# Where the first guess of rstd is made for three RMS norms of a two-layer encoder, and in how many VectorE steps it is refined

## What is computed

```python
def rmsnorm(x, g):
    xf = x.astype(jnp.float32)
    y = xf * lax.rsqrt(jnp.mean(xf * xf, axis=-1, keepdims=True) + EPS)
    return (y * g.astype(jnp.float32)).astype(x.dtype)

for i in range(DEPTH):
    h = rmsnorm(x, norm_mix[i])
    x = x + mixer(h)                       # stick-breaking (i = 0), mLSTM (i = 1)
    h = rmsnorm(x, norm_ffn[i])
    x = x + hierarchical_moe(h, ...)       # top-1 of 4 groups, top-2 of its 8 experts
return rmsnorm(x, norm_final)
```

## Time and profile before

| | us |
|---|---|
| median of 3 runs | 1743.56 |
| lowest and highest | 1743.27, 1744.08 |
| the profiled execution, its own time | 1744.14 |
| its span in the trace | 1742.4 |
| TensorE busy | 1572.3 (90%) |
| VectorE busy | 731.9 (42%) |
| ScalarE busy | 424.3 (24%) |
| mean granted TensorE clock | 0.947 |

### The profile page before, as it was taken

The page is one execution under the profiler, slowest core; times in us unless marked ns, Lnnn a source line. Parts: engine busy times, 40 slices in busy tenths (PEclk is TensorE's granted clock), DMA queues, the critical chain, the costliest instruction groups (busy, mean ns, idle before and its releaser), DMA issues.

```text
span 1742.4 us, 25494 instructions
## 1 busy us (share of the span) xinstructions
PE 1572.3 (90%) x9954; PEld 1080.8 (62%) x9954; DVE 731.9 (42%) x1170; ACT 424.3 (24%) x572; POOL 44.4 (3%) x70
## 2 busy tenths in 40 slices
PE   8999999999997789778899999999999887688776
PEld 8999999888544244324397988988864343234322
DVE  5544444443342233222364857657434332233213
ACT  6344343433000000000154333333320000000002
POOL 0010000100100000000011000000000000000000
PEclk9999999999998998889799999999999998898888
DMA  7645455578999999999954465575799999999996
GB/s 259 212 153 177 153 169 182 209 288 308 381 423 423 426 426 424 425 427 425 412 180 159 154 195 172 165 265 206 252 368 424 426 424 424 427 426 424 425 426 243
DMA packets 160785, 543.88 MB, mean 312 GB/s; under 512 B 17504, under 2 KB 34064, under 8 KB 127824
## 3 DMA queue, kind: packets, MB, share of 16 engines
q1 hardware_dynamic: 151232, 541.12, 79.8%
q10 hardware_dynamic: 9040, 0.49, 0.3%
q0 software_dynamic: 448, 1.36, 0.2%
HBM read 540.83 MB, written 2.10 MB: 312 GB/s over the span
## 4 chain that ended last, share of the span: by engine, by line
PE 68%; DMA 21%; SPq 5%; DVE 2%; issue 1%; ACT 1%; DVEq 0%; ACTq 0%
PE psum_G L755 35%; DMA ring<-in_moe_w 21%; PE psum_S L755 18%; PE psum_A L755 9%; SPq L556 5%; PE psum_T L755 5%; DVE w_lo L434 1%; ACT w_hi L430 1%; PE psum_A L762 0%; DMA x<-in_x 0%; ACT arena L1308 0%; DVE x L1855 0%; DVE h L2108 0%; PE psum_T L1009 0%; PE psum_T L762 0%
## 5 line engine op out<-in xcount | busy, mean ns | idle before, releaser
L755 PE MATMUL psum_A<-ring,arena 128*32 128x512 f32 x1984 | 289.4, 713 | 133.5 <-DMA ring<-in_moe_w 130.8
L434 DVE TENSOR_TENSOR w_lo<-ring,w_hi 128x2048 fp32r<-128x2048 f32 x126 | 289.1, 2298 | 280.5 <-ACT w_hi L430 278.3
L430 ACT CAST w_hi<-ring 128x2048 fp32r<-128x2048 f32 x127 | 241.9, 1906 | 238.5 <-PE psum_G L755 152.2
L755 PEld LDWEIGHTS psum_A<-ring,arena 128*32 128x32 f32 x1984 | 67.2, 120 | 301.6 <-issue 300.4
L1988 DVE COPY arena_two<-psum_A 128x512 f32<-128x512 f32 x64 | 44.3, 692 | 365.7 <-PE psum_T L755 336.3
L2020 DVE TENSOR_TENSOR x<-x,psum_S 128x512 f32<-128x512 f32 x128 | 88.0, 688 | 166.8 <-PE psum_S L755 166.8
L755 PE MATMUL psum_G<-xT_hi,w_hi 128*128 128x256 f32 x512 | 149.5, 292 | 0.0
L755 PE MATMUL psum_G<-xT_hi,w_lo 128*128 128x256 f32 x512 | 145.0, 283 | 0.0
L755 PE MATMUL psum_G<-xT_lo,w_hi 128*128 128x256 f32 x512 | 145.0, 283 | 0.0
L1517 ACT ACTIVATE arena<-psum_T 128x64 f32<-128x64 f32 x64 | 14.4, 224 | 473.4 <-PE psum_T L755 473.4
L755 PE MATMUL psum_G<-arena,h 128*128 128x128 f32 x1024 | 126.8, 284 | 0.0
(11 more groups left out here) (244 smaller groups left out, 2150.6 us busy)
## 6 DMA issues: line engine op xcount, KB each, us to landing
ring<-in_moe_w SPq DMA_DIRECT2D x368, 1024.0 KB, 19.1
ring<-in_ml_w_in SPq DMA_DIRECT2D x48, 1024.0 KB, 5.1
ring<-in_sb_w_in SPq DMA_DIRECT2D x47, 1024.0 KB, 5.1
ring<-in_sb_w_out SPq DMA_DIRECT2D x16, 1024.0 KB, 5.0
turned_slots<-in_moe_w SPq DMA_DIRECT2D x16, 1024.0 KB, 13.2
ring<-in_ml_w_out SPq DMA_DIRECT2D x16, 1024.0 KB, 5.1
x<-in_x SPq DMA_DIRECT2D x4, 512.0 KB, 8.2
out_x<-h SPq DMA_DIRECT2D x4, 512.0 KB, 2.7
```

The costliest lines, as they stand in the source:

```text
L430: act.copy(w_hi[:, slot_place(j), :], ring[:, slot_place(j), :]).then_inc(hi_made, 1)
L434: dve.tensor_tensor(w_lo[:, slot_place(j), :], ring[:, slot_place(j), :], w_hi[:, slot_place(j), :].bitcast(F32), ALU.subtract).then_inc(l ...
L755: return pe.matmul(dst, lhsT, rhs, start=start, stop=stop, skip_group_check=True)
```

## The change

Three tiles and one semaphore are new. For norms 1, 3 and 4:

- `early_mean(n, cols)` sums the first three chunks as before and writes two tiles: `mean_early` = sum / 2048 + eps and `half_early` = -0.5 * sum / 2048 - 0.5 * eps, and signals `early_ready`. It is now done for norm 4 as well, ahead of VectorE's last two additions.
- ScalarE makes the seed without VectorE: `seed_of_last` computes Ln(sumsq_c[:, b, 3] / 2048 + mean_early[:, b]), with the activation's scale and bias, one block at a time, right behind the square of that block, and `seed_end` takes Exp of both blocks. It no longer waits for `mean_ready`.
- VectorE writes `minus_half` = -0.5 * (mean + eps) from the last chunk and `half_early`.

For all five norms the Newton step is newton[:, b] = rstd * minus_half * rstd (one operation for each block, with `minus_half[:, b]` as a scalar for each partition; the two don't depend on each other), then rstd = (newton + 1.5) * rstd. Before it was two dependent operations on both blocks and then the last. Norms 0 and 2 keep the old hand-over to ScalarE, with one more VectorE operation for `minus_half` ahead of it.

```diff
-                if n not in (1, 3):
-                    squares_end()
-                act.wait_ge(mean_ready, n + 1)
+                squares_end()
+                act.wait_ge(mean_ready, n // 2 + 1)
                 act.activation(rstd[:, :], mean_eps[:, :], ACT.Ln)
+                seed_end()
+
+            def seed_end():
+
                 act.drain()
                 act.activation(rstd[:, :], rstd[:, :], ACT.Exp, scale=-0.5).then_inc(rstd_seed, 1)
+
+            def seed_of_last(n, b, c):
+
+                act.wait_ge(early_ready, {1: 1, 3: 2, 4: 3}[n])
+                act.activation(rstd[:, b:b + 1], sumsq_c[:, b, c:c + 1], ACT.Ln, scale=1.0 / D,
+                               bias=mean_early[:, b:b + 1])
...
             def make_rstd(n):
 
-                if n in (1, 3):
-                    dve.wait_ge(squares_done, n + 1)
-                    dve.scalar_tensor_tensor(out=mean_eps[:, :].unsqueeze(2), in0=sumsq_c[:, :, XC - 1:XC], scalar=1.0 / D,
-                                             in1=newton[:, :].unsqueeze(2), op0=ALU.mult, op1=ALU.add)
+                dve.wait_ge(squares_done, n + 1)
+                if n in (1, 3, 4):
+                    last = XC - 1
+                    dve.scalar_tensor_tensor(out=minus_half[:, :].unsqueeze(2), in0=sumsq_c[:, :, last:last + 1],
+                                             scalar=-0.5 / D, in1=half_early[:, :].unsqueeze(2), op0=ALU.mult, op1=ALU.add)
                 else:
...
+                    dve.tensor_scalar(minus_half[:, :], sumsq[:, :], -0.5 / D, -0.5 * EPS, ALU.mult, ALU.add)
+                    dve.drain().then_inc(mean_ready, 1)
+                dve.drain()
                 dve.wait_ge(rstd_seed, n + 1)
-                dve.tensor_tensor(newton[:, :], rstd[:, :], mean_eps[:, :], ALU.mult)
-                dve.drain()
-                dve.scalar_tensor_tensor(out=newton[:, :], in0=newton[:, :], scalar=-0.5, in1=rstd[:, :],
-                                         op0=ALU.mult, op1=ALU.mult)
+                for b in range(TB):
+                    dve.scalar_tensor_tensor(out=newton[:, b:b + 1], in0=rstd[:, b:b + 1], scalar=minus_half[:, b:b + 1],
+                                             in1=rstd[:, b:b + 1], op0=ALU.mult, op1=ALU.mult)
                 dve.drain()
                 dve.scalar_tensor_tensor(out=rstd[:, :], in0=newton[:, :], scalar=1.5, in1=rstd[:, :],
                                          op0=ALU.add, op1=ALU.mult)
...
                     for dc in range(4):
+                        if layer == 1 and not more and dc == XC - 1:
+                            early_mean(2, dc)
```

More of the change, by code:

```diff
@@ L193, in build @@
         newton = sb("newton", [P, TB])
+        mean_early = sb("mean_early", [P, TB])
+        half_early = sb("half_early", [P, TB])
+        minus_half = sb("minus_half", [P, TB])
         extra_f = sb("extra_f", [1, 1])
@@ L326, in build @@
         mean_ready = sem("mean_ready")
+        early_ready = sem("early_ready")
         rstd_seed = sem("rstd_seed")
@@ L1444, in last_chunk @@
                     sum_squares(b, c)
+                    if b == TB - 1:
+                        squares_end()
                     if b == 0:
@@ L1448, in last_chunk @@
                                  ).then_inc(emptied["A0"], 1)
-                squares_end()
+                    seed_of_last(2 * layer + 1, b, c)
+                seed_end()
             def first_small_loads(j):
@@ L1542, in quad @@
                                     sum_squares(b, c, moe_squares)
+                                    if c == XC - 1:
+                                        if b == TB - 1:
+                                            squares_end()
+                                        seed_of_last(4, b, c)
+                                if c == XC - 2:
+                                    act.drain().then_inc(squares_early, 1)
+                                if c == XC - 1:
+                                    seed_end()
                 with act.Fori(0, NQUAD - 1) as i:
@@ L1571, in _ @@
                 group("out", NGROUP - 1, NGROUP)
-                rstd_seed_of(2 * layer + 1)
                 experts(layer)
-            rstd_seed_of(4)
         @block.vector
@@ L1579, in make_rstd @@
             def make_rstd(n):
-                if n in (1, 3):
-                    dve.wait_ge(squares_done, n + 1)
-                    dve.scalar_tensor_tensor(out=mean_eps[:, :].unsqueeze(2), in0=sumsq_c[:, :, XC - 1:XC], scalar=1.0 / D,
-                                             in1=newton[:, :].unsqueeze(2), op0=ALU.mult, op1=ALU.add)
-                else:
-                    dve.wait_ge(squares_done, n + 1)
-                    dve.tensor_reduce(sumsq[:, :].unsqueeze(2), sumsq_c[:, :, :], AX, ALU.add)
+                dve.wait_ge(squares_done, n + 1)
[3 more added lines that the diff above has]
+                                             scalar=-0.5 / D, in1=half_early[:, :].unsqueeze(2), op0=ALU.mult, op1=ALU.add)
+                else:
+                    dve.tensor_reduce(sumsq[:, :].unsqueeze(2), sumsq_c[:, :, 0:XC], AX, ALU.add)
                     dve.drain()
                     dve.tensor_scalar(mean_eps[:, :], sumsq[:, :], 1.0 / D, EPS, ALU.mult, ALU.add)
-                dve.drain().then_inc(mean_ready, 1)
+                    dve.tensor_scalar(minus_half[:, :], sumsq[:, :], -0.5 / D, -0.5 * EPS, ALU.mult, ALU.add)
+                    dve.drain().then_inc(mean_ready, 1)
+                dve.drain()
                 dve.wait_ge(rstd_seed, n + 1)
-                dve.tensor_tensor(newton[:, :], rstd[:, :], mean_eps[:, :], ALU.mult)
-                dve.drain()
-                dve.scalar_tensor_tensor(out=newton[:, :], in0=newton[:, :], scalar=-0.5, in1=rstd[:, :],
-                                         op0=ALU.mult, op1=ALU.mult)
+                for b in range(TB):
+                    dve.scalar_tensor_tensor(out=newton[:, b:b + 1], in0=rstd[:, b:b + 1], scalar=minus_half[:, b:b + 1],
+                                             in1=rstd[:, b:b + 1], op0=ALU.mult, op1=ALU.mult)
                 dve.drain()
@@ L1602, in make_rstd, with early_mean @@
                 dve.drain().then_inc(rstd_ready, 1)
-            def early_mean(layer):
-                dve.wait_ge(squares_early, layer + 1)
-                dve.tensor_reduce(sumsq[:, :].unsqueeze(2), sumsq_c[:, :, 0:XC - 1], AX, ALU.add)
+            def early_mean(n, cols):
+                dve.wait_ge(squares_early, n + 1)
+                dve.tensor_reduce(sumsq[:, :].unsqueeze(2), sumsq_c[:, :, 0:cols], AX, ALU.add)
                 dve.drain()
-                dve.tensor_scalar(newton[:, :], sumsq[:, :], 1.0 / D, EPS, ALU.mult, ALU.add)
-                dve.drain()
+                dve.tensor_scalar(mean_early[:, :], sumsq[:, :], 1.0 / D, EPS, ALU.mult, ALU.add)
+                dve.tensor_scalar(half_early[:, :], sumsq[:, :], -0.5 / D, -0.5 * EPS, ALU.mult, ALU.add)
+                dve.drain().then_inc(early_ready, 1)
             def scaled_lo(layer, units):
@@ L1683, in common_step @@
                         if k == XC - 1:
-                            early_mean(layer)
+                            early_mean(layer, XC - 1)
                         add_chunk(layer, k)
```

## The result

The changed kernel takes 1758.64 us (median of 4 runs, 1757.56 to 1759.10), the kernel before 1743.82 (1743.27 to 1744.22) beside it: a ratio of 1.0082, with a 95% interval of 1.0070 to 1.0093. It is 15 us slower where 1 us less was forecast. The norms do about what was expected of them; the loss is elsewhere, in the stream of the experts' weights.

What follows compares the result with a forecast made beforehand. The chain of waits was taken as TensorE for 68% and DMA for 21% of the span. Norm 3's 0.50 and norm 4's 0.44 us summed to 0.94, from the median 1743.56 to 1742.6, range 1741.4 to 1744.2.

Steps and rivals of the forecast that it cites:

- The step that failed: Expert weight stream behind norm 3: loads are issued 0.50 us earlier and the whole stream ends 0.50 earlier, at 424 GB/s.
- four rivals: Norm 1 pays too 0.20 (1742.1); stall 0.14 (1743.1); half clock at norm 3 0.10 (1744.0); last quad 0.08 (1740 or 1745.5).
- three signs of being wrong: Pair of small operations over 0.5 us; fillers holding TensorE at norm 3; a later stream gap giving the half microsecond back.
- Norms 1 and 3, the rstd chain: From mean_eps or minus_half to the last Newton operation: 0.56 us less than 1.20, ends 0.47 and 0.73.
- The limit behind it: Norm 3, rstd to first experts: router product and fillers limit the gain to 0.50 us, between 0.35 and 0.54.
- Norm 1: TensorE is late behind its fillers at half clock, so cost and gain are 0 in this execution.
- Norm 4: Last square to output operations: 0.54 us less, 0.10 taken off for block 0's Ln, giving 0.44, ends 0.25 and 0.70.
- Sum: Gains over all norms: 0 + 0.50 + 0 + 0 + 0.44 = 0.94 us.
- The clock rivals: Full clock at norm 1: 0.5 us more gained, 1742.1, chance 0.20; half clock at norm 3: +0.46, 1744.0, chance 0.10.

Runs made afterwards that it cites:

- e2: The changed kernel with its three new tiles allocated behind the last one (arena), so older tiles lie where they lay before; 1743.12 us, ratio 0.9987.
- e1: The kernel before with three unused 64-byte tiles ahead of extra_f, moving h, xT, the ring and arenas by 192 bytes; 1758.09 us, ratio 1.0070.
- e3_after_again: The changed kernel measured once more without an edit, beside the kernel before; 1757.12 us, ratio 1.0076.
- e4: The kernel before with one unused 64-byte tile, a shift of 64 bytes; 1759.01 us, ratio 1.0079.
- e8: The kernel before with h and xT moved by 64 bytes and the ring by 256 in all; 1749.48 us, ratio 1.0025.

## Why the prediction was wrong

**The step that failed** is the one under which the sum was drawn up: it counted instructions and waits, and said of the stream that "the gap closes by 0.50 us, and the whole stream ends 0.50 earlier", at an unchanged 424 GB/s. The three new tiles were read in the diff and given no price. They cost 15 us. All four rivals kept the stream's rate too, so the range of 1741.4 to 1744.2 had no place for it. The evidence was at hand: the DMA share of 1.01 says that any change of a packet's duration is paid in full for half the span. Of its three signs of being wrong one was there, the fillers that held TensorE at norm 3 (0.9 us), but none of them names what cost the 15.

**Norms 1 and 3, the rstd chain: right.** Forecast 0.56 us less, measured 0.53 (1.20 to 0.67). The pair took 0.35 us, forecast 0.33: each of the two operations lasts 0.22 and the second starts 0.14 behind the first, so they overlap. The prediction set against this what the Trainium skill states in VectorE: DVE Perf Modes, section "The TRN2 errata — SBUF-src ops pay a fixed extra latency per instruction", and worked out some 0.45 by it, an estimate; this trace doesn't bear that out in full. ScalarE's Ln was mis-sized: with its per-partition addend it takes 0.29 us, not 0.20, and starts 0.15 behind the read of the square. At norm 3 that stayed hidden (the seed ended at 1282.73, `minus_half` at 1282.97).

**The limit behind it: right.** In e2, where the clock stayed up at norm 3, the mask's matmul comes 6.34 us after the start of the router product, 0.52 less than before; forecast 0.50. SyncE's issue behind the second half expert moved with it: 15.15 us behind its issue on the router product (1277.02 to 1292.17), 15.68 before (1276.80 to 1292.48).

**Norm 1: right for the clock of the trace before, and it can pay.** At half clock nothing is gained (7.76 before and in e2). At full clock it is 7.25 in e1, with the old instructions, and 6.55 in the changed kernel in both of its traces: 0.7 us.

**Norm 4: half the size.** 0.26 us (2.63 to 2.37), forecast 0.44. The term that was too small is Ln: 0.29 us long for 0.20, and 0.15 behind the read of the last square for 0.10. Therefore VectorE still waited 0.49 us for the seed, where the forecast's own times leave 0.26 (1733.09 less 1732.83). The Ln of block 0 delayed the last square by 0.14 us, near the 0.10 taken.

**Sum without the tiles.** 0.52 + 0.26 = 0.78 us where the clock is as in the trace before, forecast 0.94; e2 measured 2.3 less, with an interval of 0.3 to 4.2 us, which holds both. The part of the forecast that was about the norms stands, and it is a twentieth of what the change did.

**The clock rivals: right as mechanisms.** The half clock lies at norm 1, norm 3, both or neither from one execution to the next, with the same code (norm 3 took 7.76 in the changed kernel's first trace and 6.34 in e3_after_again's), each time behind the same TensorE pause of 0.78 us. It moves 0.5 to 1.4 us and explains none of the 15.

## What to carry to other kernels

A new tile is a change of the addresses behind it. Where the DMA engines are full, allocate small tiles behind the large ones, or round the start of the large buffers that loads go to up to 256 bytes (in all fourteen traces the stream was whole when the ring stood so, and not otherwise), and compare the start addresses of a diff's two versions before costing any instruction. When a small edit moves the time by much more than its path is long, pad the kernel before by the same bytes: that one run separates layout from logic.

## What the runs showed of the hardware that was not expected

- With the buffer that the loads go to (the ring) shifted off a 256-byte boundary, packets of 8 KB take 313.9 ns on average, not 309.1, and those of 4 KB 163.5, not 159.1: some 4.5 ns each, whatever the shift (64, 128, 192). A load's own target isn't the whole of it: at the same target bytes 482 of 512 packets were slow in e4 and 10 in e8.
- The distance between the stationary and the moving operand's buffers changes dense float32 matmuls at 1.00 clock: 288 ns or 283 for a shape of 256 columns, 5.6 us of a mixer stage of 420, and 389 ns or 394 for one of 512 columns; other distances cost up to 5.1 us in the other mixer.
- ScalarE's Ln on one column with a per-partition addend takes 0.29 us, against 0.20 for two columns without it. A pair of independent one-column VectorE operations with a per-partition scalar takes 0.35.
